# Expert layer of a two-block network: scatter and gather products moved inside the stretch loop, zero products 8 columns wide

## What is computed

```python
def moe_swiglu(x, router, wg, wu, wd):
    logits = (t @ router).astype(jnp.float32)
    top_v, top_i = lax.top_k(logits, TOP_K)          # TOP_K = 2
    top_w = jax.nn.softmax(top_v, axis=-1)
    gate = jnp.sum(jax.nn.one_hot(top_i, N_EXPERTS, dtype=jnp.float32) * top_w[..., None], axis=1)
    for e in range(N_EXPERTS):                       # 8
        y = y + gate[:, e:e + 1] * swiglu_2(t, wg[e], wu[e], wd[e])   # 1024 -> 3584 -> 1024
```

## Time and profile before

| | us |
|---|---|
| median of 3 runs | 2805.17 (2802.47 to 2805.37) |
| the profiled execution, whole | 2802.16 |
| its span, first to last instruction | 2800.4 |
| PE busy in the span | 2718.2 |
| expert layer: first sweep to the end of the last down part | 1904.19 to 2774.86 |

### The profile page before, as it was taken

The page is one execution under the profiler, slowest core; times in us unless marked ns, Lnnn a source line. Parts: engine busy times, 40 slices in busy tenths (PEclk is TensorE's granted clock), DMA queues, the critical chain, the costliest instruction groups (busy, mean ns, idle before and its releaser), DMA issues.

```text
span 2800.4 us, 80010 instructions
## 1 busy us (share of the span) xinstructions
PE 2718.2 (97%) x37718; PEld 2189.2 (78%) x37718; DVE 954.7 (34%) x1613; ACT 357.5 (13%) x731; POOL 18.5 (1%) x28
## 2 busy tenths in 40 slices
PE   8999998999999999999998999988999999999997
PEld 5777776677788766778656876658999999999996
DVE  2445445354664424554356443351000000000002
ACT  1210013100100012100251000331101000000000
POOL 1000000000000000000000000000000000000000
PEclk9999999999999999999999999999999999999999
DMA  7333422645435433444433544238999999999994
GB/s 201 136 135 135 158 83 92 218 146 172 166 129 182 136 121 121 165 153 167 142 113 106 181 145 161 86 131 344 408 412 395 403 400 396 410 394 396 411 404 194
DMA packets 260733, 619.24 MB, mean 221 GB/s; under 512 B 8886, under 2 KB 126908, under 8 KB 248156
## 3 DMA queue, kind: packets, MB, share of 16 engines
q1 hardware_dynamic: 257584, 606.13, 58.2%
q0 software_dynamic: 2400, 10.09, 1.3%
q10 hardware_dynamic: 588, 0.63, 0.1%
HBM read 615.77 MB, written 1.05 MB: 220 GB/s over the span
## 4 chain that ended last, share of the span: by engine, by line
PE 93%; DVE 4%; ACT 1%; DMA 1%; issue 1%; SPq 0%; DVEq 0%
PE ps L1789 19%; PE ps L1199 19%; PE ps L1126 14%; PE ps L1039 13%; PE ps L1804 10%; PE ps L1050 7%; PE ps L1722 2%; PE ps L1306 2%; PE ps L1776 1%; PE ps L1756 1%; DMA ring<-in_fox_w_in 1%; PE ps L1510 1%; PE ps L1520 0%; PE ps L1288 0%; DMA ring<-in_ffn_w_down 0%
## 5 line engine op out<-in xcount | busy, mean ns | idle before, releaser
L1789 PE MATMUL ps<-arena,ring 128*64 128x88 f32 x14336 | 549.7, 239 | 1.1 <-issue 1.1
L1789 PEld LDWEIGHTS ps<-arena,ring 128*64 128x64 f32 x14336 | 545.7, 138 | 4.7 <-issue 4.7
L1126 PE MATMUL ps<-ring,arena 128*128 128x512 f32 x880 | 390.3, 597 | 0.0
L1039 PE MATMUL ps<-xT,ring 128*128 128x256 f32 (+2 forms) x1664 | 368.8, 381 | 4.2 <-DMA ring<-in_fox_w_in 1.4
L1039 PEld LDWEIGHTS ps<-xT,ring 128*128 128x128 f32 (+2 forms) x1664 | 311.8, 188 | 60.6 <-issue 13.1
L1126 PEld LDWEIGHTS ps<-ring,arena 128*128 128x128 f32 x880 | 163.2, 190 | 193.2 <-issue 193.1
L2655 DVE TENSOR_TENSOR arena<-arena,ps 128x352 f32<-128x352 f32 x64 | 30.4, 475 | 727.3 <-PE ps L1789 727.3
L1199 PEld LDWEIGHTS ps<-xT,ring 128*64 128x64 f32 x2816 | 156.4, 139 | 35.0 <-issue 34.7
L1199 PE MATMUL ps<-xT,ring 128*64 128x128 f32 x2816 | 167.1, 277 | 5.3 <-DVE arena L2038 4.4
L1199 PE MATMUL ps<-arena 128*64 128x128 f32 x2816 | 169.1, 273 | 0.0
L1804 PE MATMUL ps<-arena,ring 128*64 128x88 f32 x4096 | 161.0, 239 | 1.3 <-issue 1.3
(11 more groups left out here) (450 smaller groups left out, 2255.1 us busy)
## 6 DMA issues: line engine op xcount, KB each, us to landing
ring<-in_moe_w_gate SPq DMA_DIRECT2D x64, 1792.0 KB, 11.2
ring<-in_moe_w_up SPq DMA_DIRECT2D x64, 1792.0 KB, 11.5
ring<-in_ffn_w_gate_up SPq DMA_DIRECT2D x88, 1024.0 KB, 7.7
ring<-in_moe_w_down SPq DMA_DIRECT2D x32, 2048.0 KB, 12.0
ring<-in_ffn_w_down SPq DMA_DIRECT2D x55, 1024.0 KB, 11.0
arena<-in_moe_w_down SPq DMA_DIRECT2D x32, 1024.0 KB, 9.7
arena<-in_moe_w_down SPq DMA_DIRECT2D x32, 512.0 KB, 11.8
ring<-in_fox_w_in SPq DMA_DIRECT2D x20, 768.0 KB, 6.1
```

The costliest lines, as they stand in the source:

```text
L1039: ins = pe.matmul(o, lhsT=w[:, k, c0:c0 + m], rhs=rhs[:, k, :], start=(k == 0), stop=(k == kt - 1))
L1126: return pe.matmul(ps[:, 4 + 2 * i + h, :], lhsT=h_par[:, s * S + i * P:s * S + (i + 1) * P], rhs=w[:, s, h * 512:(h + 1) * 512], start=(c ...
L1789: ins = pe.matmul(ps[h, bank, c0:c0 + CAP], lhsT=w_f[:, k, h], rhs=xe[:, 4 * kh + k, :], start=(kh == k == c0 == 0), stop=(kh == 1 and k = ...
```

## The change

- `scatter` of the previous expert moves into the stretch loop, under branches on `e > 0` and `i == 1`: half of it (token rows 0 to 127) behind sweep 1, the other half behind sweep 3. Both use banks 6 and 7 instead of 0 to 3.
- `gather` and `turn_places` move into the stretch loop, under a branch on `i == 2`, behind sweep 1. The gather is now for the next expert, not for the one after it, so that only one gather stands ahead of the expert loop and the matrix `perm` keeps two places instead of three.
- What is left between two experts is `y_turn`, with its wait for ACT's copy.
- The zero products are 8 columns wide instead of 512.
- ACT and DVE no longer loop over stretches in hardware: their four rounds are written out, with `gate_T_copy` ahead of round 2 on ACT and the two halves of `add_rows` in round 1 on DVE.

The core of the diff:

```diff
@@ ACT @@
-                    if e == 0:
-                        full()
-                    else:
-                        gate_T_copy()
+                    if e > 0:
                         y_rows_copy()
-                    with act.Fori(0, N_ST) as i:
+                    for i in range(N_ST):
+                        if i == 2:
+                            gate_T_copy()
...
@@ PE @@
-                def scatter():
-                    for i in range(TT):
+                def scatter(parts, b0):
+                    for i in parts:
                         for c in range(2):
-                            pe.matmul(ps[:, 2 * i + c, :], ...
+                            pe.matmul(ps[:, (b0 if b0 else 2 * i) + c, :], ...
...
-                pe.wait_ge(dve_to_pe, t.up("dve_to_pe"))
                 pe.wait_ge(drained_act, d_act)
-                gather(2).then_inc(full_act, 1)
                 claim(3)
...
                     for b in (4, 5):
-                        pe.matmul(ps[:, b, :], lhsT=zeros[0:1, 0:P], rhs=zeros[0:1, :], start=True, stop=False,
+                        pe.matmul(ps[:, b, 0:8], lhsT=zeros[0:1, 0:P], rhs=zeros[0:1, 0:8], start=True, stop=False,
...
                         sweep(1, 0, 2, 0, None)
+                        with pe.If(e > 0):
+                            with pe.If(i == 1):
+                                scatter((0,), 6)
+                        with pe.If(i == 2):
+                            pe.wait_ge(dve_to_pe, places_made)
+                            pe.wait_ge(drained_dve, e * 4 + d_dve)
+                            with pe.If(e < N_EXP - 1):
+                                gather(0)
+                            turn_places()
                         sweep(2, 1, 0, 1, gate_full)
                         sweep(3, 1, 2, 2, up_full)
+                        with pe.If(e > 0):
+                            with pe.If(i == 1):
+                                pe.wait_ge(drained_dve, e * 4 + (d_dve - 2))
+                                scatter((1,), 6)
                         down(4, 0, ET_A, 3)
                         down(5, ET_A, ET_B, 4).then_inc(ex_released[5], 1)
                         t.leave()
-                    with pe.If(e > 0):
-                        scatter()
-                    pe.wait_ge(dve_to_pe, t.up("dve_to_pe"))
-                    pe.wait_ge(drained_act, xe_next_read)
-                    with pe.If(e < N_EXP - 2):
-                        gather(0)
-                    turn_places()
-                    pe.wait_ge(drained_dve, e * 4 + d_dve)
                     pe.wait_ge(drained_act, yT_kept)
                     y_turn()
...
@@ DVE @@
-                    with dve.Fori(0, N_ST) as i:
-                        t.enter(i, N_ST, {"silu_ready": 2, "up_full": 2})
+                    for i in range(N_ST):
+                        if i == 1 and e > 0:
+                            add_rows((0,), 6)
...
+                        if i == 1 and e > 0:
+                            add_rows((1,), 6)
```

More of the change, by code:

```diff
@@ L360, in build @@
         cv(2, NSUB * S), cv(2, NSUB * S)
-        perm = cv(N_EXP, TT, CAP)[:, 0:3]
+        perm = cv(N_EXP, TT, CAP)[:, 0:2]
         perm_w = cv(N_EXP, TT, CAP)[:, 0]
@@ L1771, in y_turn @@
                     ins.then_inc(full_act, 1)
-                def scatter():
-                    for i in range(TT):
+                def scatter(parts, b0):
+                    for i in parts:
                         for c in range(2):
-                            pe.matmul(ps[:, 2 * i + c, :], lhsT=gate_T[0:CAP, i * P:(i + 1) * P],
+                            pe.matmul(ps[:, (b0 if b0 else 2 * i) + c, :], lhsT=gate_T[0:CAP, i * P:(i + 1) * P],
                                       rhs=y_e[0:CAP, c * 512:(c + 1) * 512], start=True, stop=True).then_inc(full_dve, 1)
@@ L1828, in moe_pass @@
                     t.enter(e, N_EXP, adds)
+                    places_made = t.up("dve_to_pe")
                     y_rows_read = e * 3 + d_act
-                    xe_next_read = e * 3 + (d_act + 1)
                     yT_kept = e * 3 + (d_act + 2)
                     for b in (4, 5):
-                        pe.matmul(ps[:, b, :], lhsT=zeros[0:1, 0:P], rhs=zeros[0:1, :], start=True, stop=False,
+                        pe.matmul(ps[:, b, 0:8], lhsT=zeros[0:1, 0:P], rhs=zeros[0:1, 0:8], start=True, stop=False,
                                   skip_group_check=True)
@@ L1859, in moe_pass @@
                 pe.wait_ge(drained_act, t.value("drained_act"))
-                scatter()
+                scatter(range(TT), 0)
                 t.up("drained_dve", 4 * N_EXP)
@@ L2611, in moe_pass @@
                 find_places(1, 0).then_inc(dve_to_pe, 1)
-                find_places(2, 1).then_inc(dve_to_pe, 1)
                 if b == 0:
                     gate_weights()
-                find_places(0, 2)
+                find_places(0, 1)
                 weigh_places(0)
@@ L2626, in moe_pass, with add_rows @@
                             ins.then_inc(x_ready, 1)
-                def add_rows(last=False):
-                    for i in range(TT):
+                def add_rows(parts=range(TT), b0=0, last=False):
+                    for i in parts:
                         for c in range(2):
@@ L2631, in add_rows @@
                             o = acc[:, i, c * 512:(c + 1) * 512]
-                            ins = dve.tensor_tensor(o, o, ps[:, 2 * i + c, :], ALU.add)
+                            ins = dve.tensor_tensor(o, o, ps[:, (b0 if b0 else 2 * i) + c, :], ALU.add)
                             if last:
@@ L2642, in moe_pass @@
                 for e in range(N_EXP):
[L2643 to L2644 removed]
                     if e > 0:
                         dve.wait_ge(places_used, t.up("places_used"))
[L2647 to L2648 removed]
+                        if e + 1 < N_EXP:
+                            find_places(0, e + 1)
                         weigh_places(e)
[L2650 to L2651 removed]
+                    for i in range(N_ST):
+                        if i == 1 and e > 0:
+                            add_rows((0,), 6)
                         for bank, c0, n in ((2, 0, ET_A), (3, ET_A, ET_B)):
```

9 lines of the change are left out of this document (removed).

## The result

The changed kernel takes 2820.48 us, the median of 5 runs (2816.93 to 2821.31), where the kernel before takes 2805.37 us on the same chip (5 runs, 2802.47 to 2808.10). The ratio is 1.0049 with a 95% interval of 1.0035 to 1.0064, so 13.7 us slower (9.8 to 18.0); the two medians by themselves are 15.1 apart. The profiled execution took 2816.93.

What follows compares the result with a forecast made beforehand. PE was taken as the bound, busy 2718.2 of 2800.4 us. Terms 7.4 - 2.9 - 1.3 + 0 + 1.5 + 0 + 4.6 gave +9.3 us, forecast 2814, range 2805 to 2820.

Steps and rivals of the forecast that it cites:

- all upper bounds: Top of the range, 2820: the sum at 15, with only 0.2 saved on the zero products.
- (a): Between experts, y_turn right behind the last down product waits for ACT's copy of yT_e: 0.93 for eight experts, +7.4 us.
- (b): Zero products of 8 columns instead of 512 save 0.36 each of eight times: -2.9 us.
- (c): Scatter and gather move: their work stays the same, two 0.64 waits for DVE go, -1.3 us.
- (d): Seams where PE's tile shape changes around moved products: 0.1 for each of about 15 more changes, +1.5 us (0 to 4.5).
- (e): Two to four new branches passed per stretch are hidden, as the sequencer is ahead of the array: 0.
- (f): First round of the stretch loop waits for its longer code, fetched in blocks: +4.6 us, bounds 0 and 6.
- rival 1: The first round hides its fetch, so its term is 0: 2808 to 2810, no change that can be told; chance 0.26.
- (2): Branches inside the stretch loop are not hidden: 0.3 to 0.6 in each of 32 stretches, about 2829; chance 0.07.
- (4): Late weights in the last stretches' sweep, relieved by spreading PE's pauses: faster, about 2798; chance 0.07.
- Rival 3: The longer stretch loop body doesn't stay resident; 31 rounds each pay 3.8 us, +118, 2930; chance 0.03.
- my "against": Objection to the longer body not staying: the loop over experts, which also jumps back, spans about the same code before and after.

Runs made afterwards that it cites:

- in halves: The changed kernel, but ACT copies yT_e in two halves, the first as soon as down part 5 has finished its bank: 2814.99 us, ratio to before 1.0026.
- alone: The kernel before with only the zero products made 8 columns wide: 2803.53 against 2807.72 us, ratio 0.9989.
- the first profile: The changed kernel's first profiled execution, nothing else altered: 2816.93 us, local (from the first gather on) 919.5.
- the quarters: The changed kernel with the scatter in four parts of one product each instead of two halves: 2820.36 us.
- the second profile: The changed kernel profiled once more, unchanged: 2819.59 against 2806.87 us for the kernel before, ratio 1.0043.
- the run with 32 products: The changed kernel with 32 never-reached products (128 instructions and a branch) behind sweep 1 of the stretch loop: 2828.49 us.

## Why the prediction was right, and where its sizes were off

The forecast was slower by 9.3 us; it was slower by 13.7 (9.8 to 18.0). Direction and mechanism held. The time lies at the upper end of the range of 2805 to 2820: by the ratio, from the median of 2805.17 that the forecast set out from, it is 2818.9, while the median of the runs, 2820.48, lies half a microsecond above. That end was added up too low: it says "all upper bounds", but with 8 x 1.1 for (a) these give 16.4 and not 15, so about 2822. The terms, measured from the first gather on:

| term | forecast | measured | from |
|---|---|---|---|
| (a) y_turn waits for ACT | +7.4 | +7.4 | 8 x 0.93 in the trace; removed in halves, 5.0 came back |
| (b) zero products | -2.9 | -2.8 | 1.50 to 1.13, seven times, 0.23 the first time; alone 0.40 per expert |
| (c) waits for DVE, gathers | -1.3 | -1.3 | no wait for DVE; one gather from the front to expert 6 |
| (d) seams | +1.5 | +5.7 | 7 x 0.49 for the scatter, 8 x about 0.28 for gather and transposes (what the other terms leave of an expert's 1.34) |
| (e) branches | 0 | 0 | rounds without moved products 25.48 |
| (f) first round | +4.6 | +2.8 and +5.9 | 32.06 and 35.2 against 29.29 and 29.4, in two executions |
| clock at the end | not seen | +1.8 and +1.5 | last scatter 6.95 and 6.66 against 3.70, partly beside DVE; its cause is open |

They add to 13.6 in the first profile, where local grew by 13.7, and to 16.4 in the second, where it grew by 16.4. The timed runs say 13.7 and 12.0 us. That in the first profile the clock at the end (+1.8) and the shorter first round (-1.8) cancel is chance.

The step that was mis-sized is (d), "I take 0.1 for each of about 15 more changes, with bounds 0 and 0.3": these changes measured 5.7, so 0.38 each, above the upper bound. The zero products, from which the 0.1 came, were read only up to the start of the sweep behind them. Behind the scatter the narrow products also take 0.15 more in all, and halving the scatter adds 0.19 of its own; the quarters confirm 0.34 for such a pair. A row that had part of it stood in the trace of before: the chain gives 17.14 for the four sweeps behind the zero products and 16.99 for the others. I had a stretch of 25.53 in the earlier trace rows, one behind zero products, and took it for any stretch.

(f) was right in kind and place: the boundary was put at record 214 + 53 = 267, and the first gap stands behind 267 records. The later gaps were shorter than the 1.5 that blocks of 6.35 give, 0.6 to 1.2. Between two executions the first round differs by 3.1 us, more than half of it by the clock, which the term did not have; so that 4.6 lies between its two measurements, 2.8 and 5.9, is in part luck.

What the prediction missed altogether is the clock: half of it under the last scatter, and in the second profile in parts of the first round too.

The rivals: the first round didn't hide its fetch (rival 1), the branches were hidden (2), late weights play no part (4): in the changed kernel the gate and up loads land in 9.9 and 9.6 us from their issue (medians of the page, 11.2 and 11.5 before), and nothing came of it. Rival 3, the longer body that doesn't stay, is not what happened, but it is real: its place is the loop over experts and not the stretch loop, and its price was 80 to 90 us and not 118. The kernel before stood fewer than 96 instructions from that edge, but more than 64. The change passed by it, as my "against" said, because it moves code inside the loop over experts and adds to it only a few branches and waits. The gather that it took out ahead of the loop widened the distance by another 128 instructions, which is why the changed kernel could take the 128 of the run with 32 products. The half of the rule in the Trainium skill, "Runtime: NRT & Kernel Launch", Instruction fetch mechanics, that gives PE room for 2048 instructions would agree with an edge between 64 and 96 instructions more, by my count of eight blocks of 256, which is off by a dozen or more; the other half, two blocks, does not: a loop that jumps back over five brought no packet.

## What to carry to other kernels

When work is moved out from between two dependent steps, ask what ran in its shadow: here a copy of 0.76 us on another engine cost nothing until the scatter and the gather left, and then 0.93 for each expert. Work of another tile shape put inside a long run of equal products pays each way in and out, and one piece cut into two pays twice; keep such work together. Before a hardware loop is made longer, find out how near its code is to the size that stays resident: the instruction queue's packets in a window of later rounds tell.

## What the runs showed of the hardware that I had not expected

- 8 products more of code that is never executed (from 16 to 24) took the kernel from 2811 to 2896 us. Every expert then read 9 packets of instructions, and PE waited up to 5.3 us for the first at the loop's head. Behind that wait the granted clock was 0.50 (zero products of 1.01 us instead of 0.53), and a third of the 90 us was slower work.
- A change between products of 128*64 and wide ones costs 0.15 in the narrow products behind it (8.65 instead of 8.49 us for two sweeps), and about 0.34 for a pair with the way in.
- Three branches between two sweeps, of which two jump, cost nothing (25.48); with a fourth that jumps the round is about 0.3 us longer, and with three that all jump about 0.1 (one run, the changed kernel with 32 skipped products).
- Under the same last four products the granted clock was 0.5 in four profiles and 1.0 in the other ten (6.66 to 7.05 us and 3.70), also between kernels that do the same work there; what decides it stays open.
- The first round of one and the same kernel took 32.1 and 35.2 us, though its first gap stands behind the same 267 records: in the slower one the granted clock fell to 0.50 twice, within the first sweep and behind the gap of 3.55 us. Behind the gap of 3.15 us in the other it stayed at 1.00.
